# Silu as one ScalarE function, a later place for the gates, and another first item in the input norm

## The reference

```python
h = rmsnorm(x, norm_g) @ w_in                 # 5648 columns
qa, ka, va, ga, qg, kg, vg, gg, lr = split(h) # 1024,256,256,1024,512,512,1024,1024,16
qa, ka = rmsnorm(qa, q_norm_g), rmsnorm(ka, k_norm_g)     # by head of 64
log_a  = log_sigmoid(lr @ w_gate_up + b_gate) / 16
oa = sink_softmax_attention(qa, ka, va)       # window of 3 chunks of 64
og = gla_scan(qg, kg, vg, log_a, state)       # recurrence, 4 heads of 128 x 256
mix = concat(oa * silu(ga), rmsnorm(og) * silu(gg))
y = x + mix @ w_out
```

## Time and profile before

| | |
|---|---|
| time, median of 3 runs | 1951.84 us |
| profiled execution | 1950.98 us, span 1949.2 us |
| PE busy | 1871.4 us, 96% |
| DVE, ACT, POOL busy | 933.9, 558.1, 498.6 us |
| granted TensorE clock, mean | 0.989 |
| DMA | 218.10 MB, mean 112 GB/s |

### The profile page before, as it was taken

One profiled execution on the slowest core, in us unless ns is written; L12 is line 12 of the kernel. 1 busy time (PEld: TensorE's weight loads), 2 busy tenths in 40 slices (PEclk: granted clock), 3 DMA queues, 4 the chain that ended last, 5 costly groups with the idle time before them and its releaser, 6 DMA issues.

```text
span 1949.2 us, 29693 instructions
## 1 busy us (share of the span) xinstructions
PE 1871.4 (96%) x10432; PEld 1705.1 (87%) x10432; DVE 933.9 (48%) x1709; ACT 558.1 (29%) x1240; POOL 498.6 (26%) x445
## 2 busy tenths in 40 slices
PE   5999999999999999999999999989999899999999
PEld 4899999978888889999888888889999888878887
DVE  7455454053344411111577777776455654353433
ACT  6211111044344310000244444440001243343332
POOL 1433333311321232332434333432323100000000
PEclk8999999999999999999999999999999999999999
DMA  6322222322332232221322323332533575575554
GB/s 223 133 68 63 67 67 73 91 76 79 101 102 75 81 93 65 73 65 51 91 79 80 88 78 94 92 107 91 154 108 107 162 242 190 166 229 183 169 185 134
DMA packets 238123, 218.10 MB, mean 112 GB/s; under 512 B 16817, under 2 KB 202673, under 8 KB 236626
## 3 DMA queue, kind: packets, MB, share of 16 engines
q1 hardware_dynamic: 170370, 174.99, 28.5%
q10 hardware_dynamic: 67696, 42.36, 8.0%
HBM read 166.82 MB, written 52.31 MB: 112 GB/s over the span
## 4 chain that ended last, share of the span: by engine, by line
PE 81%; DVE 11%; issue 3%; DMA 2%; ACT 1%; ACTq 1%; DVEq 0%; SPq 0%; POOL 0%; POOLq 0%
PE p L1590 16%; PE p L1592 15%; PE p L1591 15%; PE p L1661 6%; PE p L1663 6%; PE p L1665 6%; DVE xn L1759 4%; PE p L751 2%; PE p L506 2%; PE p L527 2%; PE p L516 1%; DMA work<-h_t 1%; PE p L762 1%; DVE xn L1757 1%; PE p L763 1%
## 5 line engine op out<-in xcount | busy, mean ns | idle before, releaser
L1590 PE MATMUL p<-x_hi,w_lo 128*128 128x384 f32 x2112 | 730.5, 346 | 0.0
L1592 PE MATMUL p<-x_hi,w_hi 128*128 128x384 f32 x2112 | 708.5, 335 | 0.0
L1591 PE MATMUL p<-x_lo,w_hi 128*128 128x384 f32 x2112 | 707.4, 335 | 0.0
L1590 PEld LDWEIGHTS p<-x_hi,w_lo 128*128 128x128 f32 x2112 | 397.8, 188 | 27.6 <-issue 25.2
L1591 PEld LDWEIGHTS p<-x_lo,w_hi 128*128 128x128 f32 x2112 | 398.2, 189 | 0.4
L1592 PEld LDWEIGHTS p<-x_hi,w_hi 128*128 128x128 f32 x2112 | 397.1, 188 | 0.0
L468 POOL TENSOR_TENSOR w_hi<-raw,small 128x512 fp32r<-128x512 f32 x176 | 185.6, 1055 | 812.3 <-PE p L1592 801.2
L473 POOL TENSOR_TENSOR w_lo<-raw,w_hi 128x512 fp32r<-128x512 f32 x176 | 228.7, 1300 | 13.8
L1839 DVE TENSOR_TENSOR w_lo<-raw,w_hi 128x512 fp32r<-128x512 f32 x192 | 131.9, 691 | 203.1 <-ACT w_hi L1541 203.1
L1541 ACT ACTIVATE w_hi<-raw 128x512 fp32r<-128x512 f32 x192 | 120.6, 631 | 240.8 <-PE p L1665 209.8
L1661 PE MATMUL p<-w_hi,x_lo 128*128 128x512 f32 x576 | 163.0, 391 | 7.7 <-DVE w_lo L1839 7.7
(11 more groups left out here) (181 smaller groups left out, 1763.5 us busy)
## 6 DMA issues: line engine op xcount, KB each, us to landing
raw<-in_w_out SPq DMA_DIRECT2D x192, 256.0 KB, 3.0
raw<-in_w_in SPq DMA_DIRECT2D x176, 256.0 KB, 3.8
h_t<-xn SPq DMA_DIRECT2D x132, 192.0 KB, 1.9
work<-h_t ACTq DMA_DIRECT2D x42, 256.0 KB, 5.0
work<-h_t SPq DMA_DIRECT2D x24, 384.0 KB, 4.9
out<-work SPq DMA_DIRECT2D x36, 256.0 KB, 5.0
work<-h_t ACTq DMA_DIRECT2D x17, 512.0 KB, 5.6
work<-in_x_prompt SPq DMA_DIRECT2D x32, 256.0 KB, 5.3
```

Source lines behind the costliest of these rows:

```text
L1590: pe.matmul(out, w_lo[:, k, :], x_hi[:, k, tok], start=(k == 0), stop=False)
L1591: pe.matmul(out, w_hi[:, k, :], x_lo[:, k, tok], start=False, stop=False)
L1592: mm = pe.matmul(out, w_hi[:, k, :], x_hi[:, k, tok], start=False, stop=(k == KT - 1))
```

## The change

- Item 0 is now the first query item. Its groups 0 and 1 run in thirds (6, 5 and 5 steps) after tiles 3 to 8; group 2 follows, with the sums of squares of groups 0 and 1 at its steps 7 and 13. Its weights are loaded behind tile 2 and split one part per tile, behind the power of tiles 1 to 4.
- The low-rank item becomes item 12 (`J_LR`), between the value items and attention. Attention's first loads are issued ahead of it, and the first attention item has the schedule of the others.
- A gate is one Silu on ScalarE and one product on VectorE, with two buffers in turn.
- From `J_GLA` to `J_LEV`, `item_late` puts `now(j, 0)` behind `unit[1]`.
- The root in linear attention is a power on GpSimd behind the next item's split. ScalarE loads a table with exponential and logarithm ahead of the gates of the decay.
- The low-rank load of the next tile is issued behind that; query and key loads ahead of the squares, with a wait for the last level.

```diff
@@ SyncE
+            for q in range(4):
+                sp.dma_start(w_raw(0, 4 * q, P), w_v[:, 4 * q:4 * q + 4, Q0:Q0 + P]).then_inc(s_w[q], 16)
...
-            for q in range(4):
-                sp.dma_start(w_raw(4 * q, RANK), w_v[:, 4 * q:4 * q + 4, LR0:LR0 + RANK]).then_inc(s_w[q], 16)
...
             sp.wait_ge(s_ss, NT)
+            sp.wait_ge(s_wready, 4)
             sp.dma_start(work[:, 2 * D_MODEL:2 * D_MODEL + M_ALL], tables).then_inc(s_tload, 16)
...
+            with sp.Fori(1, J_LR - 1) as j:
+                load_w(j + 1, j * P + (Q0 + P), P)
+                store_item(j, j * P + Q0, P)
+            load_w(J_LR, LR0, RANK)
+            store_item(J_LR - 1, (J_LR - 1) * P + Q0, P)
+            load_w(J_ATT, GQ0, P)
+            store_item(J_LR, LR0, LRR)
@@ GpSimd
-                if t == 1:
-                    split(pool, 0, RANK)
+                if 1 <= t < 5:
+                    split(pool, 0, ks=(4 * (t - 1),))
...
+        def linear_rstd(pool, t):
+            pool.wait_ge(sl_var, t + 1)
+            pool.tensor_tensor(l_rstd, l_var, mhalf[:, 0:1].to_broadcast([P, N_GLA]), ALU.pow).then_inc(sl_rs, 1)
...
                 linear_pool(pool, j - J_GLA, LEVELS, P)
                 split(pool, j + 1)
+                linear_rstd(pool, j - J_GLA)
@@ ScalarE
+                if type(t) is int and t == 1:
+                    for n in range(1, NG):
+                        act.wait_ge(s_store[n], 16 * J_LR)
...
-                for n in range(NG):
-                    self.act.wait_ge(s_store[n], 16 * J_ATT)
+                self.act.wait_ge(s_store[0], 16 * J_LR)
...
+                act.preload_act_table_set("natural_log_exp_and_others")
                 act.wait_ge(sl_log, t + 1)
...
                     self.gates(t)
+                    self.load_lr(t + 1)
...
+                    self.act.wait_ge(sl_zz, NZ * t + NZ)
+                    self.load(t + 1)
                     self.squares(t)
-                    self.rstd(t)
-                    self.load(t + 1)
...
-                act.wait_ge(s_staged, j * NG + (n + 3))
-                act.activation(tmp_a, acc[n][:, 0:TN], ACT.Exp, scale=-1.0).then_inc(s_sig, 1)
+                act.wait_ge(s_staged, j * NG + (3, 2, 4)[n])
+                act.activation(tmp_silu[n], acc[n][:, 0:TN], ACT.Silu).then_inc(s_sig, 1)
...
+            def item_late(j, before, now, unit):
+                before(j - 1, 2)
+                unit[0]()
+                unit[1]()
+                now(j, 0)
+                now(j, 1)
+                unit[2]()
...
-            item(J_GLA, nothing, item_silu, linear.tile(0))
+            item_late(J_GLA, nothing, item_silu, linear.tile(0))
@@ TensorE
+            THIRDS = [range(0, 6), range(6, 11), range(11, KT)]
             for t in range(NT):
                 turn_x(t)
-                if t % NG == 0 and t > 0:
+                if t >= NG:
                     pe.wait_ge(s_xlo, 4 * t + 4)
-                    group(0, t // NG - 1, LRR)
+                    group(0, t // NG - 1, P, ks=THIRDS[t % NG])
             pe.wait_ge(s_xlo, 4 * NT + 4)
-            group(0, NG - 1, LRR)
             pe.wait_ge(s_ones, 1)
...
+            group(0, NG - 1, P, stages={(NG - 1) * KT + 7: lambda: sum_squares(0, 0),
+                                        (NG - 1) * KT + 13: lambda: sum_squares(0, 1)})
...
+            item(J_LR, LRR)
             pe.wait_ge(s_tab, 16 * 22)
...
-            item(J_ATT, P, stages=attend_pe(pe, 0, 18))
+            item(J_ATT, P, stages=attend_pe(pe, 0))
@@ VectorE
-                    dve.tensor_scalar(tmp_a, tmp_a, 1.0, None, ALU.add).then_inc(s_schain, 1)
-                    dve.wait_ge(s_schain, base + 1)
-                    dve.reciprocal(tmp_a, tmp_a).then_inc(s_schain, 1)
-                    dve.wait_ge(s_schain, base + 2)
...
-                    dve.tensor_tensor(tmp_a[:, 0:m], acc[n][:, 0:m], tmp_a[:, 0:m], ALU.mult).then_inc(s_schain, 1)
-                    dve.wait_ge(s_schain, base + 3)
                     dve.wait_ge(s_gate[n], (j - J_GLA) * 16 + 16)
-                    done(dve.tensor_tensor(stage[n][:, 0:m], stage[n][:, 0:m], tmp_a[:, 0:m], ALU.mult))
+                    done(dve.tensor_tensor(stage[n][:, 0:m], stage[n][:, 0:m], tmp_silu[n][:, 0:m], ALU.mult))
```

More of the change, by code:

```diff
@@ L112, in project @@
         ones_r = sq_parts[:, 2 * TN:2 * TN + P]
-        lr_raw = work[:, 4 * D_MODEL:4 * D_MODEL + KT * RANK].rearrange("p (k n) -> p k n", n=RANK)
+        first_raw = work[:, 3 * D_MODEL:4 * D_MODEL]
         ss, var, rstd = small[:, 0:2], small[:, 2:3], small[:, 3:4]
@@ L284, in project, with w_raw @@
         w_v = w_in.rearrange("(k p) n -> p k n", p=P)
[L286 to L293, removed]
+        def w_raw(j, k, n):
+            buf = first_raw if type(j) is int and j == 0 else raw
+            return buf[:, k * P:k * P + 4 * n].rearrange("p (k n) -> p k n", k=4)
+        RUNS = [(J_ATT, J_GLA, GQ0, None, 0), (J_GLA, J_LEV, GA0, 0, 1),
                 (J_LEV, 1 + N_ITEMS, GG0, 1, None)]
@@ L1424, in _ @@
             pool.tensor_copy(tables_sb[:, :], work[:, 2 * D_MODEL:2 * D_MODEL + M_ALL]).then_inc(s_tables, 1)
-            with pool.Fori(2, J_GLA + 1) as j:
+            with pool.Fori(2, J_LR) as j:
+                split(pool, j)
+            split(pool, J_LR, RANK)
+            with pool.Fori(J_ATT, J_GLA + 1) as j:
                 split(pool, j)
@@ L1499, in _ @@
             attend.first()
-            with act.Fori(J_ATT, J_DEC - 1) as j:
+            item(J_ATT, nothing, nothing, attend.tile(0))
+            with act.Fori(J_ATT + 1, J_DEC - 1) as j:
                 item(j, nothing, nothing, attend.tile(j - J_ATT))
@@ L1510, in _ @@
             linear.first()
-            item(J_GLA, nothing, item_silu, linear.tile(0))
+            item_late(J_GLA, nothing, item_silu, linear.tile(0))
             with act.Fori(J_GLA + 1, J_GLA + NTP) as j:
-                item(j, item_silu, item_silu, linear.tile(j - J_GLA))
+                item_late(j, item_silu, item_silu, linear.tile(j - J_GLA))
             decode = decode_act(act, linear)
-            item(J_LEV, item_silu, item_silu, decode.levels())
+            item_late(J_LEV, item_silu, item_silu, decode.levels())
             for h in range(N_GLA):
@@ L1573, in item, with group @@
                     group(j, n, cols, norm, norm_before, stages)
-            def group(j, n, cols, norm=False, norm_before=False, stages={}):
+            def group(j, n, cols, norm=False, norm_before=False, stages={}, ks=range(KT)):
                 pe.wait_ge(s_staged, NG * j + (n + 1))
-                for k in range(KT):
+                for k in ks:
                     if n * KT + k in stages:
@@ L1716, in staging_free, with plain @@
             def staging_free(j, n):
-                dve.wait_ge(s_store[n], 16 * j)
+                if not (type(j) is int and j == 0):
+                    dve.wait_ge(s_store[n], 16 * j)
             def done(ins):
                 ins.then_inc(s_staged, 1)
-            def plain(j, n, rows=P, first=False):
+            def plain(j, n, rows=P):
                 wait_acc(dve, j, n)
-                if not first:
-                    staging_free(j, n)
+                staging_free(j, n)
                 done(dve.tensor_copy(stage[n][0:rows, :], acc[n][0:rows, 0:TN]))
@@ L1796, in _ @@
             n_gq = (GK0 - GQ0) // P
-            item(J_ATT, plain, scaled, attend.tile(0))
+            item(J_ATT, lambda j, n: plain(j, n, LRR), scaled, attend.tile(0))
             with dve.Fori(J_ATT + 1, J_ATT + n_gq) as j:
@@ L1808, in _ @@
             linear.first()
-            item(J_GLA, plain, silu, linear.tile(0))
+            item_late(J_GLA, plain, silu, linear.tile(0))
             with dve.Fori(J_GLA + 1, J_GLA + NTP) as j:
-                item(j, silu, silu, linear.tile(j - J_GLA))
+                item_late(j, silu, silu, linear.tile(j - J_GLA))
             decode = decode_dve(dve, linear)
-            item(J_LEV, silu, silu_g, decode.levels())
+            item_late(J_LEV, silu, silu_g, decode.levels())
             for h in range(N_GLA):
```

109 lines of the change are left out of this document (51 added, 58 removed).

## The result

The changed kernel takes 1890.41 us (median of 4 runs, 1889.68 to 1891.77); the kernel before took 1952.0 beside it (4 runs, 1951.67 to 1955.82). The profiled execution took 1891.77, span 1890.0, granted clock 0.996 (0.989 before). They compare one trace of each kernel, and that of the changed kernel is the longest of its four executions.

What follows compares the result with a forecast made beforehand. TensorE was taken as the bound, so only shorter or filled pauses could help. Gains of 5.7 + 6.3 + 24.8 + 4.9 + 3.1 + 3.2 = 48.0 us from 1950.98 gave 1903.0, as median 1904; range 1894 to 1923, 8 in 10.

Steps and rivals of the forecast that it cites:

- Linear attention, 24.8: Linear attention tiles: waits at the outputs, low-rank load, levels and scan go, 24.8 us gained, low end 12.
- the clock, 4.9: Linear tiles: without the pauses, three stretches at 1.2 GHz go, 3 x 1.6 = 4.9 us gained, bounds 0 and 4.9.
- L714's 3.4: Linear attention: moving the low-rank load ahead by most of an item gains 3.4 us of L714's 6.1.
- Input norm, 5.7: Input norm: query matmuls replace low-rank ones beside VectorE's normalisation, 5.7 us gained, between -2.3 and 7.7.
- rival (1): Input norm gives nothing, as TensorE at 5.0 us a tile has no room: 1910 to 1912 us, chance 0.14.
- about 0.3 in the next item: Input norm: TensorE waits 2.0 us at the second sum of squares and only about 0.3 in the next item.
- First attention item, 6.3: First attention item: waits of 3.2 for the first load and 3.1 for probabilities go, 6.3 us gained, low end 3.2.
- Decode heads, 3.1: Decode heads: four heads wait 0.8 us each behind a gate (L1073), 3.1 us gained.
- the projection's first wait, 3.2: Output projection: L1661's longest wait, 6.1 us, stands behind a gate; 3.2 us gained, between 0 and 3.6.
- Rivals (2): Linear attention keeps a wait of 1 to 2 us a tile and its slow stretches: 1912 to 1925 us, chance 0.19.
- (3): Linear items: SyncE's chain of stores and reloads makes the next weights late; slower, 1960 us at 7 us, chance 0.03.
- Rival (4): The change's waits go, but slow-clock stretches shift elsewhere: 1904 to 1909 us, chance counted within the forecast's 0.60.

Runs made afterwards that it cites:

- Run 4: Changed kernel plus six idle reciprocals on VectorE in front of the last take of each linear tile: 1925.41 us, one run.
- run 6: Changed kernel with its Silu gates but the old order, now(j, 0) between unit[0] and unit[1]: 1894.11 us.
- run 5: Kernel before with only the input norm and first attention item changed; linear attention, gates, roots and their loads as before: 1939.81 us.
- run 8: Changed kernel with the next tile's low-rank load issued behind the squares and the variance again: 1894.62 us, one run.
- Run 2: Changed kernel with GpSimd's table cast moved behind the last value item's split and the sums of squares spread further apart: 1887.12 us.
- runs 3: Changed kernel plus eight idle reciprocals a linear tile, three before VectorE's fifth level and five behind the last take: 1890.19 us, one run.
- run 1: Changed kernel with only GpSimd's table cast moved from behind the first item's split to behind the last value item's split: 1890.14 us.

## Why the prediction was off, point by point

- **Linear attention, 24.8 and the clock, 4.9: the term that was mis-sized.** The mechanism was right: the `take` no longer waits behind a reciprocal, L762, L732 and L751 are gone, no drain shows behind the tables and no wait at the roots. But I added up listed waits, as if a pause cost what the list gives it. The 29.7 measured 41.5: 8.8 more stood in no list (0.16 to 0.17 on each pause, and the slips), 1.9 more came from the clock, since not three but four stretches of 1.7 went (one lay in the first tile, ahead of its outputs: granted clock 0.83 from 935 to 945), and 1.1 more from listed waits of which the sum had left a part. Run 4 prices a pause independently (2.85 for 2.58), run 6 shows slips without an entry, run 5 that the gain is local.
- **Two forecasts inside it were wrong and cost nothing.** The power over four columns took 1.02, not 0.55, and there was room. And L714's 3.4 was put down to the earlier load; run 8 shows that the load's move is worth almost nothing in the prompt's tiles, once the root is off ScalarE.
- **Input norm, 5.7: rival (1) came true, by another mechanism.** The halves are ready at 57.7 (58.3 forecast), so VectorE's pace was right, and the splits cost it 1.4 (three normalisations of 3.12, 2.67 and 2.67 against 2.34) where 2.0 were taken. From there to the first sum it took 4.4, where 21 matmuls are 3.6. The first pause is 2.76, not 2.0, with 0.17 on top, since the subtraction took 1.52 beside a split where 0.56 was counted; the second 2.81, not 0.3; and 3.4 us at 1.2 GHz followed (0.87 from 70 to 80, 0.96 from 80 to 90), 1.7 lost. 5.7 + 0.6 - 0.7 - 0.9 - 2.7 - 1.7 = 0.3 beside a measured 0.1. The failed step is "about 0.3 in the next item": I had not looked at what GpSimd does beside that subtraction. From 29.6 to the first sum the list has no wait of TensorE, so there it was the bound, as the rival had it; but what that cost is the 0.7 by which it came late to that sum. Run 2 gives the term back, so it was a matter of step numbers and of the cast's place; and in the profiles of runs 3 and 6 most of it came without them.
- **First attention item, 6.3:** measured 7.1. The trace before has four pauses there, 6.5 with one of 0.2 at L506; at 0.17 more each they would be 7.2.
- **Decode heads, 3.1, and the projection's first wait, 3.2:** measured 4.1 and 3.1. Each of the four head pauses, listed at 0.7 to 0.8, cost 0.9 to 1.1 by starts: the same mis-sizing as in linear attention.
- **Nothing forecast for the projection itself:** 2.9. Its first wait fell from 6.12 to 3.10, and with it a stretch at 1.2 GHz. The first 20 us, before and after:

```profile
1540.00:1560.00 20.00, 13.88 (x57) 11.45 (x56) 13.63 (x18) 7.09 (x11) 0.00 (x0) 0.83 0.64 189
```

```profile
1485.00:1505.00 20.00, 16.90 (x81) 14.40 (x80) 10.79 (x16) 9.10 (x15) 0.00 (x0) 1.00 0.72 233
```

  The first nine matmuls take 3.78 before and 2.16 after, which is 1.6 of the 2.9; the rest lies later in the projection, and its cause is open. My clock term counted the linear tiles alone.
- **Rivals (2) and (3)** did not come: no wait at the `take` or the roots, no first weight wait in the linear items, and the stores in a bunch cost nothing that a list or a tile's 40.82 shows. Rival (4) is seen in part: runs 1 and 3 lost what their norm stage gained, and stretches stand elsewhere in their profiles.
- **Luck:** the range was left by only 3.6 because the 5.6 that the input norm failed to give hid half of the 11.8 by which linear attention was too small.

## What to carry to other kernels

To price a pause of an engine that issues overlapping instructions, compare starts of the same work in a tile with the pause and one without: the list of waits counts from a modelled end and here missed 30% of one tile's loss, and a fifth of the stage's gain. Replace a chain of small steps by one instruction first and reorder second: the late place without Silu made the kernel slower than it had been. When work moves into a stage, look at each of its short instructions for what the neighbour engine does at that moment, and put dependent matmul pairs as many steps apart as the chain between them lasts.

## What the hardware showed

- A VectorE subtraction with two SBUF operands beside work of GpSimd: the one that starts second bears nearly all of it. The subtraction takes 0.50 alone and the cast 2.96 alone (run 2). When the subtraction came 0.2 behind the cast they took 3.15 and 2.96. When it led by 0.8 they took 1.27 and 3.29, and its 1.27 is the split's doing, since run 1 has 1.25 without the cast.
- A table change on ScalarE cost its 1.28 and nothing around it: the load at 1032.32 began 0.02 behind the exponential before it, and the Silu 0.01 after the load's end (1033.61). The Trainium skill (ScalarE: Activation LUTs, section What ACT_TABLE_LOAD costs) adds a drain of about 1.38 to each switch; no such time shows here.
- A Silu of 128x384 takes 0.49 in the mean of 48, as an exponential of that shape before (0.49 in the mean of 48).
- Stretches at 1.2 GHz were seen behind pauses of 2 to 3 us in otherwise dense work, but not behind each: of the two pauses of 2.8 in the norm after the change only the second had one, of the eight of 2.0 to 2.1 at the outputs before three. They stand in other places from execution to execution (0.93 from 920 to 945 in runs 1 and 3, 1.00 after the change). When a given pause brings one is not settled by these runs.
